# A hybrid decoder step: first norm applied after the input projections, squares summed on VectorE

## What is computed

```python
xn = rms_norm(x, norm_mix_g)          # x * rsqrt(mean(x*x) + eps) * g
z = xn @ w_in                         # 1024 -> 3072 columns
q, k, v, hc, gb, gc = split(z)        # 512 columns each
u = gc * hc                           # conv input
conv_o = gb * conv3(u)                # depthwise, causal, width 3
```

## Time and profile before

| | |
|---|---|
| median of 3 runs | 1375.99 us (1375.83 to 1376.47) |
| the profiled execution, its own time | 1376.49 us |
| its span, first to last instruction | 1374.7 us |
| mean granted TensorE clock | 0.986 |
| PE busy | 1316.5 us (96%) |
| DVE, ACT, POOL busy | 469.3, 253.7, 518.7 us |

### The profile page before, as it was taken

The page is one execution under the profiler, slowest core; times in us unless marked ns, Lnnn a source line. Parts: engine busy times, 40 slices in busy tenths (PEclk is TensorE's granted clock), DMA queues, the critical chain, the costliest instruction groups (busy, mean ns, idle before and its releaser), DMA issues.

```text
span 1374.7 us, 20820 instructions
## 1 busy us (share of the span) xinstructions
PE 1316.5 (96%) x8476; PEld 1230.5 (90%) x8476; DVE 469.3 (34%) x860; ACT 253.7 (18%) x547; POOL 518.7 (38%) x489
## 2 busy tenths in 40 slices
PE   4899999999899999999999999999999999999994
PEld 2899898888756689999999999999999999999993
DVE  2842503123566523681131313131313131313158
ACT  4311110010277721241101010101010101010112
POOL 5433322323255323225333333333333333333343
PEclk9899999999999999999999999999999999999997
DMA  4152556434111031011111111111111111111103
GB/s 188 42 201 94 194 216 256 154 122 154 62 62 62 1 127 62 16 61 47 46 47 47 47 46 47 47 46 47 47 46 47 47 47 46 47 47 46 47 1 127
DMA packets 37940, 107.84 MB, mean 78 GB/s; under 512 B 4000, under 2 KB 16352, under 8 KB 36064
## 3 DMA queue, kind: packets, MB, share of 16 engines
q1 hardware_dynamic: 37856, 106.60, 21.6%
HBM read 95.73 MB, written 10.85 MB: 78 GB/s over the span
## 4 chain that ended last, share of the span: by engine, by line
PE 65%; DVE 5%; issue 1%; ACT 1%; POOL 1%; DVEq 0%; POOLq 0%
PE ps L503 14%; PE ps L504 14%; PE ps L505 13%; PE ps L811 6%; PE ps L812 6%; PE ps L813 6%; PE ps L621 2%; PE ps L664 2%; PE ps L645 2%; DVE work L1080 1%; DVE resid L1081 1%; POOL work L491 1%; DVE out L1081 1%; PE ps L639 1%; DVE resid L1231 0%
## 5 line engine op out<-in xcount | busy, mean ns | idle before, releaser
L503 PE MATMUL ps<-act_hi,w_hi 128*128 128x352 f32 x1608 | 523.2, 325 | 15.9 <-POOL act_lo L414 15.7
L504 PE MATMUL ps<-act_lo,w_hi 128*128 128x352 f32 x1608 | 517.0, 322 | 0.0
L505 PE MATMUL ps<-act_hi,w_lo 128*128 128x352 f32 x1608 | 517.0, 321 | 0.0
L503 PEld LDWEIGHTS ps<-act_hi,w_hi 128*128 128x128 f32 x1608 | 303.1, 189 | 31.0 <-issue 30.2
L504 PEld LDWEIGHTS ps<-act_lo,w_hi 128*128 128x128 f32 x1608 | 303.6, 189 | 0.1
L505 PEld LDWEIGHTS ps<-act_hi,w_lo 128*128 128x128 f32 x1608 | 302.8, 188 | 0.0
L383 POOL TENSOR_TENSOR gate_cell<-ones 128x1 f32<-128x1 f32 x92 | 18.4, 200 | 684.4 <-PE ps L505 488.9
L387 POOL TENSOR_TENSOR w_lo<-w_stage,w_hi 128x1024 fp32r<-128x1024 f32 x95 | 233.1, 2454 | 7.6
L1359 DVE TENSOR_TENSOR work<-ps,work 128x352 f32<-128x352 f32 x66 | 34.4, 524 | 443.4 <-PE ps L505 443.4
L811 PE MATMUL ps<-pair_hi,w_hi 128*128 128x352 f32 x504 | 163.6, 325 | 4.6 <-DVE resid L1328 3.9
L812 PE MATMUL ps<-pair_lo,w_hi 128*128 128x352 f32 x504 | 162.6, 323 | 0.0
(11 more groups left out here) (193 smaller groups left out, 1352.9 us busy)
## 6 DMA issues: line engine op xcount, KB each, us to landing
w_stage<-in_w SPq DMA_DIRECT2D x98, 512.0 KB, 3.5
resid<-in_state_k SPq DMA_DIRECT2D x8, 1792.0 KB, 8.2
v_buf<-in_state_v SPq DMA_DIRECT2D x14, 1024.0 KB, 5.0
resid<-in_xT SPq DMA_DIRECT2D x16, 528.0 KB, 7.4
out_yT<-resid SPq DMA_DIRECT2D x24, 176.0 KB, 1.8
q_d<-out SPq DMA_DIRECT2D x12, 176.0 KB, 2.0
out_kT<-out SPq DMA_DIRECT2D x12, 176.0 KB, 1.8
out_v<-out SPq DMA_DIRECT2D x16, 128.0 KB, 2.5
```

Of the source, the lines that this page charges most:

```text
L503: pe.matmul(out, hi, rhs_hi, start=first, stop=False)
L504: pe.matmul(out, hi, rhs_lo, start=False, stop=False)
L505: return pe.matmul(out, lo, rhs_hi, start=False, stop=last)
```

## The change

The norm is no longer applied to x before the projections. `act_hi`/`act_lo` hold x*g, split as whole 1056-column tiles: ACT rounds (`raw_high`), DVE forms the rest (`raw_low`). The squares are taken by ACT after that, summed over the 8 channel tiles by DVE (`add_square`), and summed over the partitions by one matmul of ones per chunk (`first_sum`), which stands behind jobs 4 and 5. 1/rms (`r_in`) is multiplied in when a projection is taken out of PSUM: q and k by DVE (`row_out`), h by DVE with 1/rms squared (`r_in2`, for h and C together), and once more for B on the conv result; the values, whose tokens lie on the partitions, by ACT with a scale per partition (`r_col`), for which PE sums the squares once more with one output column for each 128 tokens (`column_sums`). ACT no longer copies q, k or h. `QK_ORDER` becomes unit by unit, and unit 0's three jobs run tile by tile as x arrives. POOL waits for the last `raw_low` before it splits unit 1, DVE waits for that split before it sums, POOL waits for the last sum before it splits unit 2. In the conv stage `sample_weighed(0)` moves ahead of `conv_taps(1)` and `head_bias(0, 1)` ahead of `conv_gated(3)`. Cut to its core:

```diff
@@ sync
-                    sp.wait_ge(job_copied, j + 1)
+                    sp.wait_ge(row_copied, j + 1)
...
-                    sp.wait_ge(y_done, NC * KT)
+                    sp.wait_ge(raw_lo, KT)
+                    sp.wait_ge(sq_done, KT)
@@ gpsimd
+            pool.wait_ge(raw_lo, KT)
             straight(1)
+            pool.wait_ge(sq_added, KT - 1)
             straight(2)
-            for i in range(1, NC * KT, 2):
-                c, k = divmod(i, KT)
-                pool.wait_ge(hi_done, i + 1)
-                pool.tensor_tensor(act_lo[:, k, cols(c)], norm_slot(0, i), f32(act_hi[:, k, cols(c)]),
-                                   ALU.subtract).then_inc(pool_lo, 1)
@@ tensor
+            unit_ready(0)
             for k in range(KT):
-                pe.wait_ge(sq_done, k + 1)
+                pe.wait_ge(raw_lo, k + 1)
                 for c in range(NC):
-                    mm = pe.matmul(ps[:, c, 0:CH], ones[:, :], sq[k % 2][:, cols(c)], start=(k == 0), stop=(k == KT - 1))
-                mm.then_inc(ss_done, 1)
-            pe.wait_ge(mean_sq, NC)
-            for j, (n, c) in enumerate(QK_ORDER):
+                    mm = three_pass(ps[:, IN_BANK + c, 0:CH], 0, k, slice(P * k, P * k + P),
+                                    act_hi[:, k, cols(c)], act_lo[:, k, cols(c)], k == 0, k == KT - 1)
+                    if k == KT - 1:
+                        mm.then_inc(job_done, 1)
+            def first_sum(c):
+                if c < 2:
+                    pe.wait_ge(sq_added, KT - 1)
+                else:
+                    pe.wait_ge(mean_sq, 1)
+                pe.matmul(ps[:, c % 2, 0:CH], ones[:, :], ssum[:, cols(c)], start=True, stop=True).then_inc(ss_done, 1)
+            def column_sums():
+                pe.wait_ge(mean_sq, 2)
+                for tt in range(VT):
+                    m = P if tt < VT - 1 else SAMP
+                    mm = pe.matmul(ps[0:m, 1, tt:tt + 1], ssum[:, P * tt:P * tt + m], ones[:, 0:1], start=True, stop=True)
+                mm.then_inc(cols_summed, 1)
+            for j in range(NC, QK_JOBS):
+                n, c = QK_ORDER[j]
                 unit_ready(n)
-                if n == 0:
-                    pe.wait_ge(lo_done, KT // 2 * (c + 1))
-                    pe.wait_ge(pool_lo, KT // 2 * (c + 1))
                 if j >= 6:
-                    pe.wait_ge(job_copied, j - 5)
+                    pe.wait_ge(row_copied, j - 5)
                 tile_job(IN_BANK + j % 6, c, n % RING)
+                if j == 4:
+                    first_sum(0)
+                    first_sum(1)
+                if j == 5:
+                    first_sum(2)
+                    column_sums()
@@ scalar
+            def raw_high(k):
+                act.wait_ge(x_in[k], 16 if k else 32)
+                act.activation(act_hi[:, k, :], res[:, k, :], ACT.Copy, scale=g_sb[:, 0, k:k + 1]).then_inc(raw_hi, 1)
+            def raw_square(k):
+                if k >= 3:
+                    act.wait_ge(sq_added, k - 2)
+                act.activation(sq[k % 2] if k else ssum, res[:, k, :], ACT.Square).then_inc(sq_done, 1)
             for k in range(KT):
-                act.wait_ge(x_in[k], 16)
-                if k >= 2:
-                    act.wait_ge(ss_done, k - 1)
-                act.activation(sq[k % 2], res[:, k, :], ACT.Square).then_inc(sq_done, 1)
+                raw_high(k)
+            for k in range(KT):
+                raw_square(k)
             for c in range(NC):
                 take_root(0, c)
-            for c in range(NC):
-                normal_hi(0, c)
-            for j in range(QK_JOBS + V_JOBS):
+            act.wait_ge(col_mean, 1)
+            act.activation(r_col[:, :], r_col[:, :], ACT.Sqrt).then_inc(col_root, 1)
+            act.wait_ge(col_rec, 1)
...
+                act.activation(out32[0:m, j % OUT_RING, 0:256], ps[0:m, IN_BANK + i % 6, 0:256], ACT.Copy,
+                               scale=r).then_inc(val_copied, 1)
...
-            def conv_gates(p):
-                if p:
-                    act.wait_ge(c_used, NC * p)
-                else:
-                    act.wait_ge(tables_done, 1)
-                for c in range(NC):
-                    cj = 9 * p + c
-                    act.wait_ge(job_done, QK_JOBS + V_JOBS + cj + 1)
-                    copy(h_c[:, cols(c)], ps[:, conv_bank(cj), 0:CH]).then_inc(h_copied, 1)
@@ vector
+            def raw_low(k):
+                dve.wait_ge(raw_hi, k + 1)
+                dve.scalar_tensor_tensor(act_lo[:, k, :], res[:, k, :], g_sb[:, 0, k:k + 1], f32(act_hi[:, k, :]),
+                                         ALU.mult, ALU.subtract).then_inc(raw_lo, 1)
+            def add_square(k):
+                dve.wait_ge(sq_done, k + 1)
+                if k >= 2:
+                    dve.wait_ge(sq_added, k - 1)
+                dve.tensor_tensor(ssum, ssum, sq[k % 2], ALU.add).then_inc(sq_added, 1)
+            def first_rstd(c):
+                dve.wait_ge(root, c + 1)
+                chain(dve.reciprocal(r_in[:, cols(c)], r_in[:, cols(c)]))
+            def column_rstd():
+                dve.wait_ge(col_root, 1)
+                dve.reciprocal(r_col[:, :], r_col[:, :]).then_inc(col_rec, 1)
+                chain(dve.tensor_tensor(r_in2, r_in, r_in, ALU.mult))
+            dve.wait_ge(consts_in, 32)
+            chain(dve.memset(r_col[:, :], 1.0))
+            for k in range(KT):
+                raw_low(k)
+            dve.wait_ge(w_split, 4)
+            for k in range(1, KT):
+                add_square(k)
+            mean_square(0, 0)
+            mean_square(0, 1)
+            first_rstd(0)
...
+            def row_out(j):
+                dve.wait_ge(job_done, j + 1)
+                if j >= OUT_RING:
+                    dve.wait_ge(rows_stored[j % OUT_RING], 16 * (j // OUT_RING))
+                dve.tensor_tensor(out32[:, j % OUT_RING, :], ps[:, IN_BANK + j % 6, 0:CH], r_in[:, cols(QK_ORDER[j][1])],
+                                  ALU.mult).then_inc(row_copied, 1)
+            row_out(0)
+            mean_square(0, 2)
+            dve.wait_ge(cols_summed, 1)
+            dve.tensor_scalar(r_col[:, 0:VT - 1], ps[:, 1, 0:VT - 1], 1.0 / D, EPS, ALU.mult, ALU.add)
+            dve.tensor_scalar(r_col[0:SAMP, VT - 1:VT], ps[0:SAMP, 1, VT - 1:VT], 1.0 / D, EPS, ALU.mult, ALU.add
+                              ).then_inc(col_mean, 1)
+            first_rstd(1)
+            row_out(1)
+            first_rstd(2)
+            row_out(2)
+            column_rstd()
+            dve.wait_ge(made, 2)
+            row_constants()
+            tables = table_steps()
             for j in range(QK_JOBS + V_JOBS):
-                dve.wait_ge(job_copied, j + 1)
+                if NC <= j < QK_JOBS:
+                    row_out(j)
+                if j < QK_JOBS:
+                    dve.wait_ge(row_copied, j + 1)
+                else:
+                    dve.wait_ge(val_copied, j - QK_JOBS + 1)
...
+                for c in range(NC):
+                    cj = 9 * p + c
+                    dve.wait_ge(job_done, QK_JOBS + V_JOBS + cj + 1)
+                    dve.tensor_tensor(h_c[:, cols(c)], ps[:, conv_bank(cj), 0:CH], r_in2[:, cols(c)],
+                                      ALU.mult).then_inc(h_copied, 1)
...
+                chain(dve.tensor_tensor(acc_c, acc_c, r_in, ALU.mult))
...
             conv_gated(1)
+            sample_weighed(0)
             conv_taps(1)
-            sample_weighed(0)
             sample_biased(1)
...
             sample_weighed(1)
+            dve.wait_ge(s_turned, 2)
+            head_bias(0, 1)
             conv_gated(3)
             sample_kept(1)
             conv_taps(3)
             head_bias(0, 0)
-            head_bias(0, 1)
             conv_out(3, 0)
...
-QK_ORDER = [(n, c) for c in range(NC) for n in (0, 1)] + [(n, c) for n in range(2, QK_UNITS) for c in range(NC)]
+QK_ORDER = [(n, c) for n in range(QK_UNITS) for c in range(NC)]
```

More of the change, by code:

```diff
@@ L86, in build @@
         act_lo = sb("act_lo", [P, KT, TOK], F32R)
+        with nc.sbuf_tensor("early", [P, 2, 4, TOK], F32) as early:
+            pass
         pair_hi = sb("pair_hi", [P, 4, TOK], F32R)
@@ L125, in build @@
         res = resid[:, :].rearrange("p (k t) -> p k t", k=KT)
+        r_in, r_in2 = early[:, 0, 3, :], early[:, 1, 3, :]
         rstd = work[:, 0:TOK]
@@ L214, in build, with norm_slot @@
         block = ctx.enter_context(nc.Block())
[L216 to L218 removed]
+        def norm_slot(i):
+            return out32[:, 2 + i % 2, :]
         def cols(c):
@@ L834, in take_root, with normal_hi @@
                 act.wait_ge(mean_sq, NC * which + c + 1)
-                act.activation(rstd[:, cols(c)], rstd[:, cols(c)], ACT.Sqrt).then_inc(root, 1)
-            def normal_hi(which, c, ks=range(KT)):
+                r = rstd if which else r_in
+                act.activation(r[:, cols(c)], r[:, cols(c)], ACT.Sqrt).then_inc(root, 1)
+            def normal_hi(c, ks=range(KT)):
                 for k in ks:
```

(36 more changed lines are left out.)

75 lines of the change are left out of this document (29 added, 46 removed).

## The result

| | before | after |
|---|---|---|
| median of the runs | 1376.23 us (1375.83 to 1377.42, 4 runs) | 1345.76 us (1345.51 to 1347.26, 4 runs) |
| ratio | | 0.9779, 95% interval 0.9763 to 0.9796 |
| profiled execution, its span | 1376.49, 1374.7 us | 1347.26, 1345.5 us |
| PE, DVE, ACT, POOL busy | 1316.5, 469.3, 253.7, 518.7 us | 1302.2, 485.3, 237.3, 506.3 us |

A forecast was written before the change was run, and what follows sets the result against it. PE, busy 96% of the span, was taken as the bound, with waits at the start. 27.1 (start) + 1.4 - 0.1 - about 0.4 (handovers) = 28.0 us off 1376.49 gives 1348.5, said as 1348.0 for the median; range 1345.0 to 1355.0.

The forecast's parts named there:

- rival 2: Larger gain: PE at full rate a little earlier, no wait at 31.5 and at job 9; 1345.5 to 1346.5; chance 0.08.
- loss by the slow clock: At PE's start in unit 0: the first matmuls run slowly, taken as 2.1 us lost.
- `row_out(3)` done: DVE emptying a bank for job 9: done at 51.9, up to 1.04 more if POOL's cast falls there.
- wait at job 9: PE waits for DVE's `row_out(3)` to empty a bank: 0.2 to 1.3 us, taken as 0.8.
- won by `sample_channels`: Start of the kernel: job 11 ends at 64.0 instead of 91.1, 27.1 us earlier.
- won behind that: Conv stage and its end: 1.4 us from PE's wait at `sample_channels`, less 0.1, less about 0.4 for handovers.
- held by POOL's set-up: First `raw_low` beside POOL's iotas and memset: DVE held 0 to 3.4 us; nothing taken, 3.4 kept for the range.
- The 0.4 for handovers: Allowance in the total for handovers not counted: about 0.4 us off the gain.
- Rival 1: Later start: DVE held by POOL's set-up, clock falling around the sums, or late `row_out(3)`; 1350 to 1356; chance 0.27.
- Rival 3: Conv stage gives gain back: pair 1's exponential or B products late by 2 to 3 us per pair; 1352 to 1360; chance 0.08.
- Rival 4: Slower: DVE becomes the bound of the q and k jobs; 1377 to 1380; chance 0.02.
- Rival 5: Loads of later work (x, keys, values) set the end whatever PE does early; 1374 to 1377; chance 0.03.

The follow-up runs named there:

- experiment 4: Changed kernel, but unit 0's matmuls wait for the last `raw_low` instead of each for its own tile; 1353.40 us, ratio 0.9831.
- experiment 1: Changed kernel with `sample_weighed(0)` moved back behind `conv_taps(1)`; 1351.68 us, ratio 0.9824.
- experiment 10: Changed kernel rerun unedited, 1347.11 us, ratio 0.9789, beside the changed kernel with squares kept in PSUM, 1345.63 us, ratio 0.978, on one chip.
- experiment 3: Changed kernel without the three waits that make POOL's splits and DVE's sums take turns; 1353.56 us, ratio 0.9832.

## Why the prediction was right, and where it was off

1348.0 was forecast, 1345.76 measured, inside the range of 1345.0 to 1355.0 and 2.2 below the forecast, in the interval of rival 2, which had a chance of 0.08, and not in the forecast's own (1346.7 to 1349.8, 0.52). Against the profiled span, 28.0 was forecast and 29.2 won. By its own steps:

| step | predicted | in the profile after |
|---|---|---|
| first three-pass matmul | 10.3 | 10.37 |
| loss by the slow clock | 2.1 | 14 x (0.29 - 0.16) = 1.8 |
| split of unit 1 done | 22.9 | 23.29 |
| last add | 32.2 | 32.76 |
| PE waits for it | 0.7 | 0.96 |
| job 6 | 40.2 | 40.44 |
| `row_out` of 1 and 2 done | 43.5, 46.4 | 43.59, 46.41 |
| `row_out(3)` done | 51.9, up to 52.9 | 50.59 |
| wait at job 9 | 0.8 | none |
| won by `sample_channels` | 27.1 | 27.7 |
| won behind that | 1.4 - 0.1 - 0.4 = 0.9 | 1.5 |

**Right.** The whole structure: PE starts behind the first tile, is held once by the sums, and no longer waits at `sample_channels`. Experiments 4 and 1 show that the two places are what the time hangs on, by undoing a part of each. That DVE is not held by POOL's set-up was a choice between 0 and 3.4 us, and 0 came true. The rule of the Trainium skill named in the prediction agrees in its first half, which no row had shown: the iotas and the memset read no SBUF, and `raw_low` kept its 1.32.

**Off: the wait at job 9.** The step that failed priced the q copies ahead of `row_out(3)` at 0.77 each, the least in the earlier trace rows. They took 0.21 (0.42 for two); POOL was idle from 39.9 to 51.1, waiting for the weights of unit 4. The row was misread as one with POOL still. In the kernel before all eight copies stood beside a split:

```profile
64.96 0.78 DVE L1135 COPY q_blk<-out 64x32 f32<-64x32 f32 x1 [2.58 <-ACT out L831]
65.77 2.46 DVE L1135 COPY q_blk<-out 64x32 f32<-64x32 f32 x1
...
64.64 1.04 POOL L385 CAST w_hi<-w_stage 128x1024 fp32r<-128x1024 f32 x1
65.77 2.39 POOL L387 TENSOR_TENSOR w_lo<-w_stage,w_hi 128x1024 fp32r<-128x1024 f32 x1
```

The first ends 0.06 behind the cast, the second 0.07 behind the subtraction, so the least of the eight was a price with waiting in it. So `row_out(3)` was done at 50.59, and the bank that job 9 needs at 51.9 was free 1.3 us ahead; POOL's cast, feared there, came at 51.30, behind it.

**Off: small terms.** `column_sums` took 1.99 where 16-column matmuls had given 2.4. Against it stood 0.4 at the split and 0.1 at the adds. The 0.4 for handovers was never spent, and `sample_channels` itself was 0.1 shorter without its wait.

**The median against the profile.** 30.5 by the medians against 29.2 by the profiles: the profiled execution of after lies 1.5 above its median. It holds the fall near the second norm, and the spans of its other three runs fit executions without it. The forecast allowed 0.5 for the same difference in the kernel before. So the 2.2 us are 0.6 at the start, 0.6 behind it and 1.0 from this. The first two are errors of size on the right path; the third is chance: in experiment 10 the same kernel's median was 1347.11, 0.9 below the forecast.

**The rivals.** Rival 1: no second fall of the clock at the start, though PE stood for 0.96 and then ran small matmuls; but experiments 1 and 3 show that it was near, at 2.69 and 5.62 us it came. Rival 2 is where the time landed, half for its reasons: no wait at job 9, but the wait ahead of the sums was there. Rival 3: the second exponential ended at 254.5 and PE came at 255.0, 0.5 to spare where 0.8 was forecast. Rival 4: PE has no wait for a bank in any q or k job. Rival 5: no wait for a load appeared.

## What to carry to other kernels

A norm whose scale can be applied behind a projection should not stand ahead of it: what PE waits for is then one tile of x, and the sum has until the first bank must be emptied; and when the start is a chain over several engines, ask what is late next before shortening a link: the warm clock was worth nothing here while the additions held the chain, and behind them the next split was late. Where DVE and POOL work side by side, additions of DVE with one input in PSUM ran free of POOL, while with two inputs in SBUF both engines slowed down (and copies and scalings from SBUF to SBUF were held too); moving the data to PSUM beat taking turns, by 0.8 and 1.5 us.

## What the runs showed of the hardware that was not expected

- A wait of PE costs more than its length when the granted clock falls behind it. In these runs it fell after waits of 2.44, 2.69, 3.5 and 5.62 us, not after 0.96, 1.40, 1.46 and 1.51, and after 2.25 to 2.31 in some executions and not in others. One fall near the second norm costs 1.6 us.
- At the very start the matmuls are 0.29 us apart for about 4 us while the granted clock in the rows reads 1.00; 30 matmuls of ones ahead remove it. There the spacing tells the clock, not the column.
- An add of 352 columns from PSUM took 0.435 us in a run of 21 without a gap (9.14/21), against 0.525 for the duration of a product of the same form standing alone. The first is from start to start, the second the length of one row.
- Beside POOL's splits both sides suffer: seven adds 9.43 to 17.05, a cast 1.05 to 2.08, a subtraction 2.40 to 3.28. The single rows of experiment 3 show one engine standing until the other's instruction is over, in both directions. Two inputs in SBUF are not needed for that: line 1280 (one input in SBUF, 128x1024) stands until the subtraction is over, and a copy of 64x32 takes 0.21 alone and 2.46 beside a subtraction.
